# Prompt attention: the causal mask added in PSUM by VectorE, and a unit's reciprocal placed behind the next unit's maximum

## The chip, the core and the metric

The kernel runs on one core of a Trainium2 chip. The metric is the device time of one execution in microseconds; the figure of a kernel is the median of its runs. The core has five engines with queues of their own, which are released by semaphores: TensorE (PE, with its weight loads shown apart as PEld), VectorE (DVE), ScalarE (ACT), GpSimd (POOL) and SyncE (SP, which here starts DMAs).

## What is computed

One inference step of a decoder trunk of two layers, for a prompt of 512 tokens and for 8 samples of 8 tokens. The change touches one piece of it: the attention of the prompt over its own keys. With 512 tokens both the selected-block branch (all 8 blocks of 64 are selected) and the window branch (window 512) are plain causal attention:

```python
s = jnp.einsum('bcqgnd,bcsgd->bcqgns', qb, kb) * (HEAD_DIM ** -0.5)
p = masked_softmax(s, mask)      # mask: key position <= query position

def masked_softmax(s, mask):
    s = jnp.where(mask, s.astype(jnp.float32), -jnp.inf)
    m = jnp.max(s, axis=-1, keepdims=True)
    e = jnp.exp(s - m)
    return e / jnp.maximum(jnp.sum(e, axis=-1, keepdims=True), 1e-30)
```

There are 8 query heads in 2 groups (v = 0, 1) of 4 (g), and head size 64. The probabilities are multiplied by a gate per head and token, and the two branches are summed.

## The kernel before

The program is a row of blocks; all engines meet at the end of each. Each of the two layers has one block for the prompt attention. Its work is cut into NA = 32 units, `AU`: query tile t (128 queries, from 3 down to 0), branch b (0 selected, 1 window) and g (0 to 3). A unit holds both head groups v, and t + 1 key tiles, so w = 512, 384, 256 or 128 keys for t = 3, 2, 1, 0; eight units in a row have the same t. The units are numbered 0 to 31 here.

Every engine has its own hand-written order, one pass of a loop per unit n:

- PE: `scores(n)`, two fp32 matmuls (L1346) into banks 2(n mod 2) and 2(n mod 2) + 1, then two bf16 matmuls of the identity with the causal mask (L1348), which add the mask onto the last 128 columns of each bank; then `turn_probs(n - 3)`, which transposes the probabilities of the unit three back (L1359, LAG = 3); then `values(n - 4)`, the product with V (L1373). `scores(n)` waits for the exponentials of unit n - 2, which free its banks. `turn_probs(m)` waits for the scaled probabilities of m, and for the copies out of the transposes of m - 1.
- DVE: the negated maximum of both groups in one reduction (L1448), once the scores are there; then the copy of the transposes of unit n - 3 for v = 1 (L1405); then the wait for both exponentials of unit n, and the reciprocal of their sums (L1453).
- ACT: two exponentials with their sums (L1424) behind the maximum; then the copy of the transposes of n - 3 for v = 0 (L1405); every eighth unit the copy of the finished output (L1433).
- POOL: behind the reciprocal, two multiplications of the probabilities by reciprocal and gate (L1323).
- SP in this block only starts loads for the next one.

`cst` is the tile of constants in SBUF; `ident16` and `causal16` are bf16 views of it. `step(engine, instruction, name)` issues an instruction that raises a semaphore at its end, and makes the same engine wait for it before it goes on. The names in rows: `bank` is PSUM, and `R` is a large tile that holds queries, keys, probabilities and their sums.

Of the kernel before, what the change touches and what calls it, by code (L numbers as in the profile page):

```python
# [20 lines left out]

F32 = mybir.dt.float32
F32R = mybir.dt.float32r
BF16 = mybir.dt.bfloat16
I32 = mybir.dt.int32
U32 = mybir.dt.uint32
ALU = mybir.AluOpType
# [3 lines left out]
P = 128  # L31
# [13 lines left out]
NKV = 2  # L45
# [18 lines left out]
NEG = -1e30  # L64
# [5 lines left out]
CONST_W = {}  # L70


def _halved(a):

    return (np.asarray(a, np.float32).view(np.uint32) >> 16).astype(np.uint16).view(np.float32)


def _constants():

    cols = []  # L80

    def put(name, a):
        a = np.asarray(a, np.float32).reshape(a.shape[0], -1)
        full = np.zeros((P, a.shape[1]), np.float32)
        full[:a.shape[0]] = a
        CONST_W[name] = (sum(c.shape[1] for c in cols), a.shape[1])
        cols.append(full)

    i = np.arange(P)
    put("ident", np.eye(P))  # L90
    put("ones", np.ones((P, P)))
    put("ones64", (i[:, None] // HD == i[None] // HD))

    put("ident16", _halved(np.eye(P)))
    put("causal16", _halved(np.where(i[None] > i[:, None], NEG, 0.0)))
    put("hgmask", (i[:, None] // CH == i[None] // CH) & (i[:, None] <= i[None]))
    j = np.arange(NS)
    put("hgmask8", (j[:, None] // DT == j[None] // DT) & (j[:, None] <= j[None]))
    pos = np.concatenate([np.arange(SEQ), PAST + np.tile(np.arange(DT), NB), np.zeros(P - NS)]).astype(np.float32)
    inv = (np.float32(10000.0) ** (-np.arange(HD // 2, dtype=np.float32) / np.float32(HD // 2))).astype(np.float32)  # L100
    ang = (pos[:, None] * inv[None]).astype(np.float32).reshape(TT, P, HD // 2).transpose(1, 0, 2)
    put("cos", np.cos(ang.astype(np.float64)))
    put("sin", np.sin(ang.astype(np.float64)))
    c = np.arange(NCP)
    q = np.arange(SEQ).reshape(NT, P).T
    seen = (c[None, None] * CST + 2 * CST - 1 <= q[:, :, None]) & (c < NCP - 1)
    put("cmpneg", np.where(seen, 0.0, NEG))
    put("cmp01", seen)

    rows = np.arange(P)  # L110
    par_, hd, t = rows // (NH * DT), rows // DT % NH, rows % DT
    own = np.arange(NB // 2)[None, :, None, None] * 2 + par_[:, None, None, None] == np.arange(NB)[None, None, :, None]
    new = own & (np.arange(DT)[None, None, None] <= t[:, None, None, None])
    put("newneg", np.where(new, 0.0, NEG))
    put("winneg", np.where(np.arange(DT)[None] > t[:, None], 0.0, NEG))
    put("groupsum", (rows[:, None] // (NG * DT) == rows[None] // (NG * DT)) & (t[:, None] == t[None]))

    put("rowsel", j[:, None] % (2 * DT) == (par_ * DT + t)[None])
    put("pair", j[:, None] // (2 * DT) == np.arange(NB // 2)[None])
    put("head", hd[:, None] == np.arange(NH)[None])  # L120
    put("blkidx", np.tile(np.arange(16), (P, 1)))
    put("batch", (i[:, None] // DT % 4 == np.arange(4)[None]))
    n = np.arange(N)
    put("scan", np.tile(np.where(n < SEQ, n % CH != 0, (n - SEQ) % DT != 0), (P, 1)))
    return np.concatenate(cols, axis=1)
# [10 lines left out]
def build(nc, x_prompt, x_sample, cache_nsa_kv, cache_win_kv, state_hgrn, page_table,  # L136
# [4 lines left out]
    with ExitStack() as ctx:  # L141
# [56 lines left out]
        def const(name, rows=P):  # L198
            o, w = CONST_W[name]
            return cst[0:rows, o:o + w]  # L200

        ident, ones, ones64 = const("ident"), const("ones"), const("ones64")
        ident16, causal16 = const("ident16").bitcast(BF16), const("causal16").bitcast(BF16)

        G_ATTN, G_MLP, G_HG, G_KC, P_B1, P_LBA, P_OM, P_LNOM, P_HB = 0, 8, 16, 17, 18, 22, 26, 30, 34

# [319 lines left out]
        def layer(l):  # L526
# [663 lines left out]
            NA = len(AU)  # L1190
# [108 lines left out]
            with nc.Block() as block:  # L1299
# [26 lines left out]
                @block.tensor  # L1326
                def _(pe):
                    for u, (k, t) in enumerate(TURNS):
                        r, n, dst = turn_views(k, t)
                        if u >= 4:  # L1330
                            pe.wait_ge(sem(f"turn_kept{u % 2}"), (u - 4) // 2 + 1)
                        for g in range(n):
                            src = (q_tok, QR)[k][0:r, t, g * P:(g + 1) * P] if k < 2 else ktok[g][0:r, t, :]
                            ins = pe.transpose(bank[u % 4][:, g * r:(g + 1) * r], src, ident[0:r, 0:r])
                        ins.then_inc(sem("turned"), 1)
                    for i in range(2):
                        pe.wait_ge(sem(f"turn_kept{i}"), kept_before(len(TURNS), i))

                    def scores(n):
                        t, b, g = AU[n]  # L1340
                        w = (t + 1) * P
                        if n >= 2:
                            pe.wait_ge(sem("probs_made"), 2 * (n - 1))
                        for v in range(NKV):
                            k = slice(v * HD, (v + 1) * HD)
                            pe.matmul(bank[2 * (n % 2) + v][:, 0:w], QT[k, g, t * P:w], KT[k, b, 0:w], start=True, stop=False)  # L1346
                        for v in range(NKV):
                            ins = pe.matmul(bank[2 * (n % 2) + v][:, t * P:w], ident16, causal16,  # L1348
                                            start=False, stop=True)
                        ins.then_inc(sem("scored"), 1)  # L1350

                    def turn_probs(n):
                        t, b, g = AU[n]
                        for v in range(NKV):
                            pe.wait_ge(sem("probs_scaled"), 2 * n + v + 1)
                            if n >= 1:
                                pe.wait_ge(sem(f"probsT_kept{v}"), n)
                            for j in range(t + 1):
                                ins = pe.transpose(bank[4 + v][:, j * P:(j + 1) * P],  # L1359
                                                   probs[n % 4][:, v * 512 + j * P:v * 512 + (j + 1) * P], ident)  # L1360
                            ins.then_inc(sem(f"probs_turned{v}"), 1)

                    def values(n):
                        t, b, g = AU[n]
                        i = NT - 1 - t
                        if b == 0 and g == 0 and i >= 2:
                            pe.wait_ge(sem("o_kept"), i - 1)
                        for v in range(NKV):
                            pe.wait_ge(sem(f"probsT_kept{v}"), n + 1)
                        for j in range(t + 1):  # L1370
                            for v in range(NKV):

                                ins = pe.matmul(bank[6 + i % 2][v * HD:(v + 1) * HD, g * P:(g + 1) * P],  # L1373
                                                vtok[b][:, j, v * HD:(v + 1) * HD],
                                                probsT[n % 2][:, v * 512 + j * P:v * 512 + (j + 1) * P],
                                                start=(b == 0 and g == 0 and j == 0), stop=(b == 1 and j == t),
                                                skip_group_check=True)
                        ins.then_inc(sem("valued"), 1)

                    for n in range(NA + LAG + 1):  # L1380
                        if n < NA:
                            scores(n)
                        if LAG <= n < NA + LAG:
                            turn_probs(n - LAG)
                        if n > LAG:
                            values(n - LAG - 1)
# [50 lines left out]
                def _(dve):  # L1437
# [5 lines left out]
                    for n in range(NA + LAG):  # L1443
                        if n < NA:
                            w = (AU[n][0] + 1) * P
                            dve.wait_ge(sem("scored"), n + 1)
                            both = psum[:, n % 2 * 1024:n % 2 * 1024 + 1024].rearrange("p (v k) -> p v k", v=NKV)[:, :, 0:w]
                            dve.tensor_reduce(nmax[:, 2 * n:2 * n + 2], both, AX, ALU.max, negate=True).then_inc(sem("maxed"), 1)  # L1448
                        if n >= LAG:
                            keep_probsT(nc.vector, n - LAG, 1)  # L1450
                        if n < NA:
                            dve.wait_ge(sem("probs_made"), 2 * n + 2)
                            dve.reciprocal(rinv[:, 2 * n:2 * n + 2], rsum[:, 2 * n:2 * n + 2]).then_inc(sem("rsum_inverted"), 1)  # L1453

            att_scope.close()
            cmp_scope = ExitStack()
# [1021 lines left out]
```

## Time and profile before

| | us |
|---|---|
| median of 3 runs | 2060.67 |
| lowest and highest of them | 2057.65, 2062.05 |
| the profiled execution, its whole time | 2054.93 |
| its span, first to last instruction | 2053.1 |
| its attention of layer 0, first scores to the last unit's | 265.7 to 344.2 |
| its attention of layer 1, first scores to the last unit's | 1276.0 to 1354.4 |

The profiled execution lasted 2054.93 us, 1.8 us over its span and 5.7 us under the median. A row of the timeline gives the start, the duration, the engine, the line, the operation with its tiles, and in brackets how long the engine sat idle before it and what ended that. PE rows merge several matmuls; the end of a matmul is modelled. One fp32 matmul shows as two records.

### The profile page before, as it was taken

The page shows a single profiled execution, that of the slowest core. Times are in us where ns is not written, and L with a number is a line of the kernel's source. Part 1 is how long each engine was busy: PE and PEld are TensorE (multiplying, and loading weights), DVE is VectorE, ACT ScalarE, POOL GpSimd, SP SyncE. Part 2 cuts the span into 40 slices and gives each one's busy share as a digit, 9 for nine tenths or more (in the row PEclk, how much of TensorE's full clock was granted, in tenths as well). Part 3 has the DMA queues.
Part 4 walks back from the last instruction along what each step waited for, and adds up shares of the span by engine and source line. Part 5 has one row for each costly group of instructions (what it writes and reads, how often), then busy time and mean ns, then how long its engine had stood idle before and what let it go on. Part 6 is the DMA issues. An engine that isn't in the chain of part 4 may idle for free. (4 is left out here: it accounts for less than half of the span.)

```text
span 2053.1 us, 38910 instructions
## 1 busy us (share of the span) xinstructions
PE 1905.8 (93%) x15789; PEld 1785.9 (87%) x15789; DVE 1138.6 (55%) x1899; ACT 828.1 (40%) x1809; POOL 692.3 (34%) x470
## 2 busy tenths in 40 slices
PE   6999798988799999999999997989887999999998
PEld 6999555988599999999999984668875999999998
DVE  4589655454455555555528886555535454545454
ACT  4594355353534131313146923544435341313130
POOL 2325435240043333333323542443201333333331
PEclk8999888999999999999999997999999999999999
DMA  4220520432522222222222223222254222222221
GB/s 155 86 80 23 164 66 9 117 93 70 158 83 83 83 83 84 82 87 83 78 85 84 63 73 104 58 64 67 83 154 111 83 71 93 78 92 81 85 82 48
DMA packets 200638, 175.80 MB, mean 86 GB/s; under 512 B 11356, under 2 KB 198030, under 8 KB 200334
## 3 DMA queue, kind: packets, MB, share of 16 engines
q1 hardware_dynamic: 200354, 173.30, 27.7%
q8 instruction: 126, 2.06, 0.4%
q14 instruction: 50, 0.41, 0.1%
q10 hardware_dynamic: 108, 0.03, 0.0%
HBM read 162.67 MB, written 10.62 MB: 84 GB/s over the span
## 5 line engine op out<-in xcount | busy, mean ns | idle before, releaser
L427 POOL TENSOR_TENSOR WX<-RAW,WX 128x2048 fp32r<-128x2048 f32 (+2 forms) x48 | 222.4, 4634 | 523.0 <-ACT WX L423 523.0
L2391 DVE TENSOR_TENSOR sq<-sq 128x288 f32<-128x288 f32 x128 | 156.9, 1231 | 196.8 <-ACT sq L2360 196.8
L427 POOL TENSOR_TENSOR m_wl<-RAW,m_wh 128x2048 fp32r<-128x2048 f32 x36 | 166.5, 4624 | 285.1 <-ACT m_wh L423 285.1
L439 PE MATMUL bank<-UH,m_wl 128*128 128x288 f32 x640 | 188.7, 295 | 0.0
L438 PE MATMUL bank<-UL,m_wh 128*128 128x288 f32 x640 | 188.7, 295 | 0.0
L437 PE MATMUL bank<-UH,m_wh 128*128 128x288 f32 x640 | 188.6, 295 | 0.0
L439 PE MATMUL bank<-UH,WX 128*128 128x288 f32 x576 | 170.0, 295 | 0.0
L438 PE MATMUL bank<-UL,WX 128*128 128x288 f32 x576 | 169.8, 295 | 0.0
L437 PE MATMUL bank<-UH,WX 128*128 128x288 f32 x576 | 169.6, 295 | 0.0
L2410 DVE TENSOR_TENSOR OT<-bank,rstd 128x288 f32<-128x288 f32 x128 | 58.2, 455 | 183.2 <-PE bank L439 183.2
L2413 DVE TENSOR_TENSOR XT<-XT,OT 128x288 f32<-128x288 f32 x128 | 156.3, 1221 | 4.4
L423 ACT ACTIVATE WX<-RAW 128x2048 fp32r<-128x2048 f32 (+1 forms) x48 | 92.0, 1917 | 160.8 <-PE bank L439 150.8
L1616 PE MATMUL bank<-FTS,W1S 128*128 128x256 f32 (+1 forms) x512 | 155.9, 305 | 0.0
L437 PE MATMUL bank<-m_ah,m_wh 128*128 128x288 f32 x512 | 151.3, 296 | 0.0
L439 PE MATMUL bank<-m_ah,m_wl 128*128 128x288 f32 x512 | 151.0, 295 | 0.0
L438 PE MATMUL bank<-m_al,m_wh 128*128 128x288 f32 x512 | 151.0, 295 | 0.0
L1618 PE MATMUL bank<-FTS,W1S 128*128 128x256 f32 (+1 forms) x512 | 150.5, 294 | 0.0
L1619 PE MATMUL bank<-FTS,W1S 128*128 128x256 f32 (+1 forms) x512 | 150.1, 293 | 0.0
L2360 ACT ACTIVATE sq<-bank 128x288 f32<-128x288 f32 x128 | 52.5, 410 | 233.7 <-PE bank L439 216.9
L423 ACT ACTIVATE m_wh<-RAW 128x2048 fp32r<-128x2048 f32 x36 | 68.7, 1908 | 166.7 <-PE bank L439 166.7
L439 PE MATMUL bank<-m_ah,WX 128*128 128x288 f32 x448 | 132.2, 295 | 0.0
L438 PE MATMUL bank<-m_al,WX 128*128 128x288 f32 x448 | 132.0, 295 | 0.0
(386 smaller groups left out, 5829.3 us busy)
## 6 DMA issues: line engine op xcount, KB each, us to landing
RAW<-in_w_up SPq DMA_DIRECT2D x32, 1024.0 KB, 5.4
RAW<-in_w_down SPq DMA_DIRECT2D x32, 1024.0 KB, 5.2
RAW<-in_w_in SPq DMA_DIRECT2D x20, 1024.0 KB, 5.3
R<-in_cache_nsa_kv SPq DMA_DIRECT2D x128, 64.0 KB
HT<-in_cache_nsa_kv SPq DMA_DIRECT2D x128, 64.0 KB, 2.6
RAW<-in_w_in SPq DMA_DIRECT2D x6, 1056.0 KB, 5.4
R<-in_cache_nsa_kv SPq DMA_DIRECT2D x48, 128.0 KB, 2.8
out<-R SPq DMA_DIRECT2D x10, 512.0 KB, 5.0
```

The source lines that it names most:

```text
L423: act.activation(S.granule(S.wh, i, w), S.granule(S.raw, i, w), ACT.Copy).then_inc(sem(S.name + "w_hi"), 1)
L427: eng.tensor_tensor(S.granule(S.wl, i, w)[:, chunks], S.granule(S.raw, i, w)[:, chunks], S.granule(S.wh, i, w)[:, chunks].bitcast(F32), AL ...
L437: pe.matmul(out, wh[:, c, cols], ah[:, c, n], start=(c == 0), stop=False)
L438: pe.matmul(out, wh[:, c, cols], al[:, c, n], start=False, stop=False)
L439: ins = pe.matmul(out, wl[:, c, cols], ah[:, c, n], start=False, stop=(c == KC - 1))
L1616: pe.matmul(out, W1H[:, s, c, cols], xh, start=first and (h == 0 or CU[w][1] == 0), stop=False, skip_group_check=True)
L1618: pe.matmul(out, W1H[:, s, c, cols], xl, start=False, stop=False, skip_group_check=True)
L1619: ins = pe.matmul(out, W1L[:, s, c, cols], xh, start=False, stop=last, skip_group_check=True)
L2360: act.activation(relu[n % 4], bank[2 + u % 6][:, 0:HALF], ACT.Relu).then_inc(sem("m_relued"), 1)
L2391: dve.tensor_tensor(relu[n % 4], relu[n % 4], relu[n % 4], ALU.mult).then_inc(sem("relu_squared"), 1)
L2410: dve.tensor_tensor(grown[n % 2], bank[2 + u % 6][:, 0:HALF], rstd[:, halves(s)], ALU.mult).then_inc(sem("m_added"), 1)
L2413: dve.tensor_tensor(x, x, grown[n % 2], ALU.add).then_inc(sem("m_grown"), 1)
```

## The change

The bf16 mask matmuls are gone from PE. In their place DVE adds an fp32 mask to the last 128 columns of both banks, in PSUM, before the maximum, with a wait for its own end between the two. The reciprocal of unit n - 1 now stands behind the maximum of unit n, and ahead of the copy of the transposes, where before the reciprocal of unit n closed its own pass. The constants keep their total width.

```diff
-    put("ident16", _halved(np.eye(P)))
-    put("causal16", _halved(np.where(i[None] > i[:, None], NEG, 0.0)))
+    put("causal", np.where(i[None] > i[:, None], NEG, 0.0))
...
                         for v in range(NKV):
                             k = slice(v * HD, (v + 1) * HD)
-                            pe.matmul(bank[2 * (n % 2) + v][:, 0:w], QT[k, g, t * P:w], KT[k, b, 0:w], start=True, stop=False)
-                        for v in range(NKV):
-                            ins = pe.matmul(bank[2 * (n % 2) + v][:, t * P:w], ident16, causal16,
-                                            start=False, stop=True)
+                            ins = pe.matmul(bank[2 * (n % 2) + v][:, 0:w], QT[k, g, t * P:w], KT[k, b, 0:w], start=True, stop=True)
                         ins.then_inc(sem("scored"), 1)
...
+                            own = both[:, :, w - P:w]
+                            step(dve, dve.tensor_tensor(own, own, const("causal").unsqueeze(1).to_broadcast([P, NKV, P]), ALU.add),
+                                 "dve_done")
                             dve.tensor_reduce(nmax[:, 2 * n:2 * n + 2], both, AX, ALU.max, negate=True).then_inc(sem("maxed"), 1)
+
+                        if 1 <= n <= NA:
+                            dve.wait_ge(sem("probs_made"), 2 * n)
+                            dve.reciprocal(rinv[:, 2 * n - 2:2 * n], rsum[:, 2 * n - 2:2 * n]).then_inc(sem("rsum_inverted"), 1)
                         if n >= LAG:
                             keep_probsT(nc.vector, n - LAG, 1)
-                        if n < NA:
-                            dve.wait_ge(sem("probs_made"), 2 * n + 2)
-                            dve.reciprocal(rinv[:, 2 * n:2 * n + 2], rsum[:, 2 * n:2 * n + 2]).then_inc(sem("rsum_inverted"), 1)
```

DVE at the start of the attention of layer 0, before: maximum and reciprocal of units 0 to 2, then maximum, copy and reciprocal of unit 3.

```order
L1448 TENSOR_REDUCE R_0<-bank 128x2
L1453 RECIPROCAL R_0<-R_0 128x2
L1448 TENSOR_REDUCE R_0<-bank 128x2
L1453 RECIPROCAL R_0<-R_0 128x2
L1448 TENSOR_REDUCE R_0<-bank 128x2
L1453 RECIPROCAL R_0<-R_0 128x2
L1448 TENSOR_REDUCE R_0<-bank 128x2
L1405 COPY R_0<-bank 128x512
```

The same place after the change (L1438 the mask, L1440 the maximum, L1444 the reciprocal, L1393 the copy):

```order
L1438 TENSOR_TENSOR bank<-bank,cst 128x2x128
L1440 TENSOR_REDUCE R_0<-bank 128x2
L1438 TENSOR_TENSOR bank<-bank,cst 128x2x128
L1440 TENSOR_REDUCE R_0<-bank 128x2
L1444 RECIPROCAL R_0<-R_0 128x2
L1438 TENSOR_TENSOR bank<-bank,cst 128x2x128
L1440 TENSOR_REDUCE R_0<-bank 128x2
L1444 RECIPROCAL R_0<-R_0 128x2
L1438 TENSOR_TENSOR bank<-bank,cst 128x2x128
L1440 TENSOR_REDUCE R_0<-bank 128x2
L1444 RECIPROCAL R_0<-R_0 128x2
L1393 COPY R_0<-bank 128x512
```

Unit 1's maximum no longer stands behind unit 0's reciprocal, and so not behind unit 0's exponentials.

PE in the attention of layer 0, units 4 and 5, before (scores, mask, transposes, values):

```order
L1346 MATMUL bank<-R_0 128x512 x2
L1348 MATMUL bank<-cst 128x128 x2
L1359 MATMUL bank<-cst,R_0 128x128 x8
L1373 MATMUL bank<-R_0 64x128 x8
L1346 MATMUL bank<-R_0 128x512 x2
L1348 MATMUL bank<-cst 128x128 x2
```

And after:

```order
L1337 MATMUL bank<-R_0 128x512 x2
L1347 MATMUL bank<-cst,R_0 128x128 x8
L1361 MATMUL bank<-R_0 64x128 x8
L1337 MATMUL bank<-R_0 128x512 x2
```

Scores, transposes and values keep their order; only the mask matmuls are missing.

## Rows read from the trace of the kernel before

**Rows 1.** The page, part 1: engine, busy us (share of the span), instructions.
```profile
PE 1905.8 (93%) x15789; PEld 1785.9 (87%) x15789; DVE 1138.6 (55%) x1899; ACT 828.1 (40%) x1809; POOL 692.3 (34%) x470
```

**Rows 2.** Line L1348 alone: count, duration in ns min/median/max, first and last start.
```profile
L1348 PE MATMUL bank<-cst x128: 218/229/315, 266.8 to 1354.9; 128*128 128x128 bf16 x128
```

**Rows 3.** The timeline, layer 0, units 5 to 8 (t = 3), all engines.
```profile
284.28 1.13 PE L1346 MATMUL bank<-R 64*128 64x512 f32 x4
285.34 0.29 PE L1348 MATMUL bank<-cst 128*128 128x128 bf16 x2
285.59 1.06 PE L1359 MATMUL bank<-cst,R 128*128 128x128 f32 x8
285.66 1.22 DVE L1448 TENSOR_REDUCE R<-bank 128x2 f32<-128x1024 f32 x1 [0.50 <-PE bank L1348]
286.80 0.68 DVE L1405 COPY R<-bank 128x512 f32<-128x512 f32 x1
286.92 0.69 ACT L1424 ACTIVATE R<-bank,R 128x512 f32<-128x512 f32 x1 [1.47 <-DVE R L1448]
...
288.26 0.59 ACT L1405 ACTIVATE R<-bank 128x512 f32<-128x512 f32 x1
...
288.97 0.86 PEld L1359 LDWEIGHTS bank<-cst,R 128*128 128x128 f32 x8 [0.19 <-issue]
289.00 1.07 PE L1359 MATMUL bank<-cst,R 128*128 128x128 f32 x8
...
291.02 0.92 PE L1346 MATMUL bank<-R 64*128 64x384 f32 x4
```

**Rows 4.** The same, units 29 to 31 (t = 0).
```profile
341.14 0.49 PE L1346 MATMUL bank<-R 64*128 64x128 f32 x4
...
341.89 0.42 DVE L1448 TENSOR_REDUCE R<-bank 128x2 f32<-128x256 f32 x1
...
343.05 0.27 ACT L1405 ACTIVATE R<-bank 128x128 f32<-128x128 f32 x1
...
343.46 0.43 PE L1359 MATMUL bank<-cst,R 128*128 128x128 f32 x2
...
344.19 0.49 PE L1346 MATMUL bank<-R 64*128 64x128 f32 x4
```

**Rows 5.** DVE adds a constant to PSUM data, then reduces it behind a wait for itself.
```profile
403.42 0.42 DVE L1935 TENSOR_TENSOR R<-bank,cst 128x256 f32<-128x256 f32 x1
403.87 0.42 DVE L1936 TENSOR_REDUCE R<-R 128x8 f32<-128x256 f32 x1
```

**Rows 6.** The timeline, layer 0, the first units and unit 5's scores.
```profile
269.94 1.20 DVE L1448 TENSOR_REDUCE R<-bank 128x2 f32<-128x1024 f32 x1
...
272.65 0.17 DVE L1453 RECIPROCAL R<-R 128x2 f32<-128x2 f32 x1 [1.51 <-ACT R L1424]
...
272.68 2.08 PE L1346 MATMUL bank<-R 64*128 64x512 f32 x4 [1.45 <-ACT R L1424]
272.74 1.20 DVE L1448 TENSOR_REDUCE R<-bank 128x2 f32<-128x1024 f32 x1
...
275.54 1.20 DVE L1448 TENSOR_REDUCE R<-bank 128x2 f32<-128x1024 f32 x1
...
280.87 1.13 PE L1346 MATMUL bank<-R 64*128 64x512 f32 x4
```

**Rows 7.** The page, part 5: busy us, mean ns of one, idle before and its releaser.
```profile
L2413 DVE TENSOR_TENSOR XT<-XT,OT 128x288 f32<-128x288 f32 x128 | 156.3, 1221 | 4.4
```

**Rows 8.** Stretches of the span: length, busy us of PE, PEld, DVE, ACT, POOL, then granted TensorE clock, DMA.
```profile
345.00:346.00 1.00, 0.72 (x6) 0.36 (x6) 0.65 (x2) 0.60 (x3) 0.79 (x2) 1.00 0.00 0
346.00:347.00 1.00, 0.49 (x2) 0.32 (x2) 0.17 (x1) 0.51 (x4) 0.50 (x2) 0.84 0.00 0
347.00:348.00 1.00, 1.00 (x6) 0.50 (x6) 0.29 (x1) 0.14 (x1) 0.38 (x1) 0.50 0.06 16
543.60:547.00 3.40, 2.45 (x20) 1.83 (x20) 0.00 (x0) 3.40 (x7) 0.00 (x0) 1.00 0.83 187
```

More of the change, by code:

```diff
@@ L23 @@
 F32R = mybir.dt.float32r
-BF16 = mybir.dt.bfloat16
 I32 = mybir.dt.int32
@@ L70 @@
 CONST_W = {}
-def _halved(a):
-    return (np.asarray(a, np.float32).view(np.uint32) >> 16).astype(np.uint16).view(np.float32)
 def _constants():
@@ L202, in build @@
         ident, ones, ones64 = const("ident"), const("ones"), const("ones64")
-        ident16, causal16 = const("ident16").bitcast(BF16), const("causal16").bitcast(BF16)
         G_ATTN, G_MLP, G_HG, G_KC, P_B1, P_LBA, P_OM, P_LNOM, P_HB = 0, 8, 16, 17, 18, 22, 26, 30, 34
```

## The prediction, made before the changed kernel ran

> **What bounds the kernel now.** I read the page's busy shares first. PE is busy for 93% of the span and DVE for 55% [rows 1]. That invites the reading that anything taken off PE and given to DVE is a gain, so the next question is whether PE is what ends the waits in the one stage that changes. The stage is the attention, twice some 78 us from the first scores to the last unit's scores, 32 units each.
>
> The timeline of four units with t = 3 answers it [rows 3]. Follow one unit. Its scores start at 284.28. Its mask matmuls start at 285.34 and end at 285.63, and the maximum starts 0.03 later, at 285.66. It ends at 286.88; the exponentials start at 286.92. ACT's copy of the transposes stands behind them in its queue: 288.26 to 288.85. The next transposes on PE wait for that copy, since it frees their bank, and start at 289.00, 0.15 after its end, with 0.19 us of idle before the weight load. Transposes and values run to 291.02, where the scores two units on start. So there is a **loop over two units**: scores, mask, maximum, exponentials, ACT's copy, then transposes and values on PE. It takes 4.72 + 2.02 = 6.74 us, 3.37 per unit. PE's own work is just under it: its waits in the loop are of the order of 0.1 us.
>
> With t = 0 it is the same [rows 4]: scores at 341.14, maximum at 341.89, ACT's copy 343.05 to 343.32, the transposes 0.14 later at 343.46, and the scores two units on at 344.19: 3.05 us for two units. PE and the loop are nearly in balance, and the loop is the longer one. What counts is therefore the latency from scores to exponentials, not the work on PE.
>
> **The change part by part.**
>
> *The mask matmuls go.* There are 128 records of about 0.23 us, one for each v of 64 units [rows 2]. On PE a unit gives back the 0.25 us from the mask's start to the transposes' start (285.34 to 285.59) [rows 3]. On the loop it is a little less: DVE can start 0.04 after the end of the scores' own matmuls. For t = 3 these end at 284.28 + 1.13 = 285.41, so DVE starts at 285.45 in place of 285.66, 0.21 earlier. For t = 0 they end at 341.63, so DVE starts at 341.67 in place of 341.89, 0.22 earlier [rows 4]. I take 0.215.
>
> *The add comes.* It is 256 fp32 elements per partition, one input from PSUM and one from the constants. The trace has that instruction in another stage: 0.42 us, and the reduction that waits for it starts 0.45 after its start [rows 5]. That one writes to SBUF; no DVE row of before writes to PSUM. From above, the dearest row for adding so little is 1.22 us for 288 elements, with both inputs in SBUF while POOL is at work [rows 7]; the add has one input in PSUM, so I take the row of the same shape, 0.45. From below, if the maximum could start as early as the copy does behind a maximum that it need not wait for, 0.08 before its end (286.80 against 286.88) [rows 3], the pair would cost 0.42 - 0.08 = 0.34. The loop thus grows by 0.45 - 0.215 = **0.235 us per two units**, with ends of 0.125 and about 1.0.
>
> A rule bears on the lower end. The Trainium skill, "VectorE: DVE Perf Modes", section "The DRAIN you can't avoid", says that a semaphore between chained VectorE operations costs nothing extra. Here a waited-for pair has a gap of 0.03 and a pair without a wait an overlap of 0.08, so the rows differ from the rule by 0.11. By the rule the loop would grow by 0.125.
>
> *What the freed PE time is worth.* In the new loop PE has 0.25 less per unit and the loop is 0.12 more, so PE waits longer and nothing is gained. DVE stays clear: for t = 3 it has 0.45 + 1.22 + 0.17 + 0.68 = 2.52 us of 3.49; for t = 0 0.45 + 0.42 + 0.17 + 0.29 = 1.33 of 1.64.
>
> *The reciprocal moves.* In the steady part the old wait was over by the time the next scores came, so nothing is gained there, but with scores 0.2 earlier it would have begun to hold the add; the move keeps that from happening. Queued behind the new wait on unit n - 1's exponentials is only DVE's copy, and these exponentials ended long before. POOL gets its reciprocal about 2 us later for t = 3 and 1 us later for t = 0; the transposes that need its result come three units later, so this is covered.
>
> *The head of the stage* is where the move pays. In units 0 to 3 the maxima start at 269.94, 272.74 and 275.54, 2.80 apart: maximum, exponentials, reciprocal, maximum in a row, the last reciprocal starting at 272.65 [rows 6]. Now unit n + 1's maximum runs beside unit n's exponentials. By hand: unit 0's maximum starts at 267.35, unit 1's at 269.03 (was 269.94), unit 2's at 271.7 (272.74), and unit 3's scores at 271.75 in place of 272.68. They ran at half the clock (2.08 us where 1.13 is usual); at that price they end at 273.83, and unit 3's maximum starts at 274.3 in place of 275.54. Its exponentials and ACT's copy end at 277.6, so the second set of transposes starts at 277.75, and unit 5's scores come at 279.8 to 280.3 in place of 280.87 [rows 6]. One loop later, at unit 7, 0.35 to 0.85 is left: I take 0.6. Had the clock been full, it would be up to 1.5.
>
> *Sum for a layer.* From unit 7 to unit 31 are 12 loops: 12 x 0.235 = 2.8. The last unit's own mask adds 0.24. Less 0.6 at the head: +2.45. The drain of the last three units and the next stage, which starts at a meeting of all engines, shift with it. SP's loads end long before. Two layers: **+4.9 us**. On the profiled execution that is 2054.93 + 4.9 = 2059.8; on the median, 2060.67 + 4.9 = 2065.6. A measurement of this kernel can tell about 0.2% (4.1 us) from no change, so this is just past it.
>
> **The rivals.**
>
> *PE is the bound after all.* Then each unit gives back 0.25: 64 x 0.25 = 16 us, 2044.7. For it speaks 93% [rows 1]; against it the start 0.15 after ACT's copy, at t = 3 and t = 0 alike [rows 3, 4].
>
> *The head gives back the rest.* With full clock at the head, 1.5 us come back per layer: 2 x (3.04 - 1.5) = 3.1, so 2063.7. The pair at 0.34 gives the like: 12 x 0.125 + 0.13 - 0.6 = 1.0 per layer, 2062.7. Both are within 0.2%. That second figure is what the page's rule, named above, would give.
>
> *The clock falls among the units of t = 0.* PE now has some 1.15 us of work in 1.64. Before, the granted clock fell to half behind two microseconds with 0.72 and 0.49 of PE busy [rows 8]. At half clock PE needs 2.1 us for such a unit, 0.45 more than the loop. This decides once PE's share there is too low. Eight units in two layers: 16 x 0.45 = 7.2 more, 2072.8. Against it: a stretch of 3.4 us with 2.45 busy kept the full clock [rows 8].
>
> *The add into PSUM is dear.* At 1.22 plus 0.03 the loop grows by 1.03, 0.8 more than taken: 25 loops x 0.8 = 20 us, 2085. It is decided by the add's own duration, above about 0.5.
>
> **How the numbers follow.** The forecast has 0.62, with a range of its own of 2062.5 to 2069; a third of that chance, 0.21, is within 0.2%. The head or the cheap pair 0.16, the clock 0.12, the dear add 0.04, PE as the bound 0.06. Faster by over 0.2%: 0.06. Within 0.2%: 0.21 + 0.16 = 0.37. Slower: 0.41 + 0.12 + 0.04 = 0.57. The range leaves out PE as the bound and the dear add (0.10) and some tails: 2059 to 2073.5.
>
> **What the new profile would show.** The add at 0.42 with the maximum 0.45 behind its start; the scores of t = 3 some 6.97 us apart over two units and those of t = 0 3.29; the transposes still 0.14 behind ACT's copy, with longer PE waits; maxima at the head nearer than 2.8; unit 31's scores about 2.2 us later. PE spacings that shrink by 0.25 per unit would make the prediction wrong, as would a granted clock of half in the units of t = 0.

## The result, and the profile after

The changed kernel takes 2067.92 us in the median of 8 runs (2063.28 to 2074.19), the kernel before 2059.57 (8 runs, 2056.84 to 2065.17). The ratio is 1.0037 with a 95% interval of 1.0021 to 1.0053, so the change costs 7.6 us by the ratio (4.3 to 10.9); the two medians are 8.4 apart. The forecast was 4.9 more: the direction and the range were right, the size was under the measured one.

The page of the profiled execution (2063.28 us, span 2061.5), part 1, against [rows 1]:

```profile
span 2061.5 us, 38718 instructions
PE 1896.4 (92%) x15661; PEld 1783.1 (86%) x15661; DVE 1157.5 (56%) x1963; ACT 828.8 (40%) x1809; POOL 693.5 (34%) x470
```

PE has 128 instructions and 9.4 us fewer, DVE 64 instructions and 18.9 us more. Next the add and the maximum, each line alone (count, ns min/median/max, first and last start):

```profile
L1438 DVE TENSOR_TENSOR bank<-bank,cst x64: 411/433/433, 270.8 to 1361.0; 128x256 f32<-128x256 f32 x64
L1440 DVE TENSOR_REDUCE R<-bank x64: 424/824/1226, 271.3 to 1361.5; 128x2 f32<-128x1024 f32 x16, 128x2 f32<-128x768 f32 x16, 128x2 f32<-128x512 f32 x16, 128x2 f32<-128x256 f32 x16
```

The loop over two units at t = 3, to be read against [rows 3]: units 6 to 8 of layer 0.

```profile
285.80 1.13 PE L1337 MATMUL bank<-R 64*128 64x512 f32 x4
...
286.98 0.43 DVE L1438 TENSOR_TENSOR bank<-bank,cst 128x256 f32<-128x256 f32 x1 [0.76 <-PE bank L1337]
...
287.45 1.22 DVE L1440 TENSOR_REDUCE R<-bank 128x2 f32<-128x1024 f32 x1
...
288.59 0.15 DVE L1444 RECIPROCAL R<-R 128x2 f32<-128x2 f32 x1
...
288.71 0.69 ACT L1412 ACTIVATE R<-bank,R 128x512 f32<-128x512 f32 x1 [1.17 <-DVE R L1440]
...
290.05 0.59 ACT L1393 ACTIVATE R<-bank 128x512 f32<-128x512 f32 x1
290.75 0.86 PEld L1347 LDWEIGHTS bank<-cst,R 128*128 128x128 f32 x8 [0.76 <-POOL R L1314]
290.79 1.07 PE L1347 MATMUL bank<-cst,R 128*128 128x128 f32 x8
...
292.81 0.92 PE L1337 MATMUL bank<-R 64*128 64x384 f32 x4
```

The add starts 1.18 us after the scores' start, the maximum 0.47 later, ACT's copy ends at 290.64, and the transposes start 0.15 behind it. The releaser printed beside them is POOL, but POOL's result of that time belongs to a later unit; what ended 0.15 before is the copy, as in [rows 3]. From 285.80 to 292.81 are 7.01 us, where it was 6.74. At t = 0 the scores of units 28 and 30 start at 344.18 and 347.49, 3.31 apart, where [rows 4] has 3.05.

Where the time went, by stretches of the span (the length, then busy us of PE, PEld, DVE, ACT, POOL, the granted TensorE clock, DMA). The changed kernel: the stage ahead of layer 0's attention, that attention from first to last scores, its drain up to the next stage's first matmul, and the same two for layer 1.

```profile
218.22:269.64 51.42, 38.76 (x380) 28.19 (x381) 34.34 (x105) 18.47 (x75) 16.84 (x25) 0.73 0.42 128
269.64:349.41 79.77, 65.34 (x577) 41.66 (x577) 54.28 (x120) 46.04 (x153) 36.16 (x59) 1.00 0.16 45
349.41:357.97 8.56, 5.56 (x34) 2.87 (x33) 2.98 (x12) 3.75 (x14) 3.15 (x9) 0.66 0.00 0
1280.69:1360.50 79.81, 65.39 (x576) 41.69 (x577) 54.27 (x120) 46.08 (x153) 36.20 (x59) 1.00 0.16 44
1360.50:1369.11 8.61, 5.61 (x34) 2.86 (x33) 2.60 (x11) 3.67 (x13) 3.08 (x9) 0.61 0.01 3
```

And the same five of the kernel before:

```profile
218.40:265.73 47.33, 34.82 (x380) 25.05 (x381) 34.27 (x105) 18.43 (x75) 16.80 (x25) 0.82 0.45 138
265.73:344.19 78.46, 73.89 (x638) 45.98 (x639) 43.90 (x89) 45.89 (x153) 36.39 (x60) 0.96 0.16 45
344.19:352.63 8.44, 5.89 (x36) 2.99 (x34) 2.74 (x11) 3.81 (x14) 2.69 (x8) 0.65 0.01 2
1276.00:1354.44 78.44, 73.95 (x638) 46.00 (x638) 43.96 (x89) 45.77 (x151) 36.39 (x60) 0.96 0.16 45
1354.44:1361.38 6.94, 4.33 (x36) 2.53 (x35) 2.73 (x11) 3.92 (x15) 2.70 (x8) 1.00 0.01 4
```

The two attentions with their drains are 1.31 + 0.12 + 1.37 + 1.67 = 4.5 us longer. The spans differ by 8.4. The first row alone is 4.1 longer, in code that is the same in both kernels: it ran at a granted clock of 0.73 here and 0.82 there. Later stretches add and take smaller amounts. The same stage ahead of layer 1's attention, first in the changed kernel and then in the one before, shows that this goes with the execution and not with the kernel:

```profile
1232.84:1280.69 47.85, 35.33 (x381) 25.11 (x381) 34.32 (x105) 18.47 (x75) 16.74 (x25) 0.82 0.44 137
1227.41:1276.00 48.59, 35.94 (x381) 25.68 (x381) 34.28 (x105) 18.44 (x75) 16.74 (x25) 0.79 0.43 134
```

In layer 1 the changed kernel is the quicker one there, and its own two layers differ by 3.6 us.

### The profile page after: what moved, and what is told of

Same layout as the page of the kernel before. It is cut to its first block and busy times, and to the rows that moved or that the text cites. A ratio compares the mean times of both kernels' runs of the same rounds, so it can differ in the third digit from the quotient of the medians.

```text
span 2061.5 us, 38718 instructions
## 1 busy us (share of the span) xinstructions
PE 1896.4 (92%) x15661; PEld 1783.1 (86%) x15661; DVE 1157.5 (56%) x1963; ACT 828.8 (40%) x1809; POOL 693.5 (34%) x470
```

## The experiments

The theory: the attention runs at the pace of the loop over two units (scores, mask, maximum, exponentials, ACT's copy, transposes, values), and what the change does to that latency is what it costs. The rivals: PE's work is the bound; the order of the reciprocal or the missing PE work (by way of the clock) makes the difference; DVE's own load is the bound.

"Attention" in the table is first to last scores in layers 0 and 1, "drain" from the last scores to the next stage's first matmul, both of the profiled execution, and "head" is unit 0 to unit 5 in layer 0. The ratio is to the kernel before as timed beside the same kernels, so the median of the kernel before is given as a range.

| kernel | median us | ratio to before (95%) | head | attention | drain |
|---|---|---|---|---|---|
| before | 2059 to 2061 | 1 | 15.14 | 78.46, 78.44 | 8.44, 6.94 |
| changed | 2067.92 | 1.0037 (1.0021 to 1.0053) | 13.06 | 79.77, 79.81 | 8.56, 8.61 |
| recip_only | 2054.55 | 0.9967 (0.9956 to 0.9979) | 12.23 | 75.58, 75.58 | 7.97, 6.94 |
| mask_only | 2074.97 | 1.0083 (1.0068 to 1.0098) | 16.79 | 84.02, 84.50 | 8.27, 8.92 |
| ones_dve | 2072.42 | 1.0061 (1.0046 to 1.0075) | 14.48 | 83.87, 83.86 | 8.29, 8.06 |
| add_twice | 2082.34 | 1.0116 (1.0099 to 1.0132) | 15.34 | 88.37, 88.63 | 9.42, 9.41 |
| no_mask | 2051.38 | 0.9954 (0.9932 to 0.9975) | 11.80 | 72.51, 73.63 | 6.73, 6.74 |
| act_first_dve | 2043.73 | 0.9932 (0.9918 to 0.9946) | 12.85 | 69.29, 69.29 | 6.54, 6.52 |
| act_first_pe | 2044.31 | 0.9929 (0.9916 to 0.9942) | 13.34 | 71.41, 73.14 | 6.68, 6.69 |
| act_first_recip_pe | 2042.37 | 0.9917 (0.9900 to 0.9934) | 11.47 | 69.54, 69.54 | 6.29, 6.28 |

**The reciprocal alone (recip_only).** From the kernel before:

```diff
+                        if 1 <= n <= NA:
+                            dve.wait_ge(sem("probs_made"), 2 * n)
+                            dve.reciprocal(rinv[:, 2 * n - 2:2 * n], rsum[:, 2 * n - 2:2 * n]).then_inc(sem("rsum_inverted"), 1)
                         if n >= LAG:
                             keep_probsT(nc.vector, n - LAG, 1)
-                        if n < NA:
-                            dve.wait_ge(sem("probs_made"), 2 * n + 2)
-                            dve.reciprocal(rinv[:, 2 * n:2 * n + 2], rsum[:, 2 * n:2 * n + 2]).then_inc(sem("rsum_inverted"), 1)
```

> The kernel before with one edit: a unit's reciprocal stands behind the next unit's maximum, the mask stays on PE. Loop theory: the steady part does not change (3.37 us per unit at t = 3), only the head of the attention gets shorter, by about 2 us at unit 7 in each layer, since the maxima no longer stand behind the exponentials of the unit before: 4 us less in all, 2056. Rival, that the move buys nothing on its own and the changed kernel's shorter head comes from the missing mask matmuls: 0. The rest of the changed kernel's loss over the attention's own would then lie in the mask's move alone.

It is 6.8 us faster than before (4.3 to 9.1), where 4 was expected. The attentions are 2.9 us shorter each. DVE at the head:

```profile
268.49 2.50 DVE L1448 TENSOR_REDUCE R<-bank 128x2 f32<-128x1024 f32 x2 [1.53 <-PE bank L1348]
271.24 0.17 DVE L1451 RECIPROCAL R<-R 128x2 f32<-128x2 f32 x1 [0.24 <-ACT R L1424]
272.64 1.23 DVE L1448 TENSOR_REDUCE R<-bank 128x2 f32<-128x1024 f32 x1 [1.24 <-PE bank L1348]
```

Two maxima run back to back, and the reciprocal comes behind them; in [rows 6] each maximum had to wait for the reciprocal. The scores of units 5 and 7 are still 6.74 apart, so the steady part is unchanged, and the gain in the attentions is in the first units: unit 7 comes 18.97 us after unit 0, before 21.88. The rival (no gain of its own) falls.

Not all of these 2.9 us are the order's. In the kernel before, unit 3's scores ran at half clock, 2.08 us in [rows 6]; here they took 1.13:

```profile
272.59 1.13 PE L1346 MATMUL bank<-R 64*128 64x512 f32 x4
```

At full clock on both sides the order is worth 1.87 us a layer: unit 7 comes 19.70 after unit 0 in layer 0 of act_first_pe and 17.83 in act_first_recip_pe, two kernels further down that differ in the reciprocal alone. Layer 1 of act_first_pe, with unit 3's scores at 2.08 us, needs 21.43. So about 1.9 of the 2.9 is the order, as expected, and about 1.0 the clock. The kernel before shows the half clock at unit 3 in both layers and recip_only in neither; whether the order brings that about was not shown.

**The mask alone (mask_only).** The changed kernel with the reciprocal put back:

```diff
-                        if 1 <= n <= NA:
-                            dve.wait_ge(sem("probs_made"), 2 * n)
-                            dve.reciprocal(rinv[:, 2 * n - 2:2 * n], rsum[:, 2 * n - 2:2 * n]).then_inc(sem("rsum_inverted"), 1)
                         if n >= LAG:
                             keep_probsT(nc.vector, n - LAG, 1)
+                        if n < NA:
+                            dve.wait_ge(sem("probs_made"), 2 * n + 2)
+                            dve.reciprocal(rinv[:, 2 * n:2 * n + 2], rsum[:, 2 * n:2 * n + 2]).then_inc(sem("rsum_inverted"), 1)
```

> The changed kernel with the reciprocal back in its old place, so only the mask moves. Loop theory: the loop over two units grows by 0.26 us (12 times in a layer, 3.1 us), the four units at the head each carry the add's 0.47 in a row with maximum, exponentials and reciprocal (1.9 us), and for t = 0 that row, 0.47 + 0.42 + 0.04 + 0.70 + 0.05 + 0.17 = 1.85 us per unit, becomes longer than half the loop of 1.65 (with t = 1 about 2.4 us in a layer). Together 7.4 us a layer, 15 us in all: 2074. Rival, the order of the reciprocal does not matter for the steady part: 3.1 + 1.9 a layer, 10 us in all.

It is 17 us slower than before (14 to 20), where 15 was expected and 10 by the rival. The attentions alone do not bear the theory out so well: they are 5.6 and 6.1 us longer, for 7.4 expected and 5.0 by the rival. The head costs the 1.9 that was put for it (unit 7 comes 23.79 us after unit 0, before 21.88), and from unit 7 to unit 31 it is 3.6 and 4.1 us more than before, for 5.5 and 3.1. Its units of t = 0 show the row of work that the rival left out:

```profile
343.54 0.17 DVE L1446 RECIPROCAL R<-R 128x2 f32<-128x2 f32 x1 [0.53 <-ACT R L1412]
343.62 0.41 DVE L1438 TENSOR_TENSOR bank<-bank,cst 128x256 f32<-128x256 f32 x1
...
344.07 0.42 DVE L1440 TENSOR_REDUCE R<-bank 128x2 f32<-128x256 f32 x1
```

DVE waits for the exponentials, inverts, and only then begins the next unit's add. The last steps of layer 0 show its length: the scores of units 29 to 31 come 1.83 apart, for 1.85 expected, where two units of the changed kernel take 3.31. But this row rules only part of the stage. From unit 7 to unit 31 it adds 0.5 us in layer 0 and 1.0 in layer 1 to the changed kernel's time (60.22 and 60.71 against 59.71 and 59.76), not 2.4, and in layer 1 the clock had part in it: over the last 8 us before unit 31 it was 0.84. So of the change's two halves the mask costs about 17 us and the reciprocal's move gives back 6.8 alone and about 9 once the add is there; of these 9, 3.7 us a layer are at the head (23.79 against 20.06 at unit 7), where mask_only again ran unit 3's scores at half clock.

**Its cost apart from PE (ones_dve).** From recip_only, with the mask still on PE:

```diff
+                            own = both[:, :, w - P:w]
+                            step(dve, dve.tensor_tensor(own, own, const("ones").unsqueeze(1).to_broadcast([P, NKV, P]), ALU.mult),
+                                 "dve_done")
                             dve.tensor_reduce(nmax[:, 2 * n:2 * n + 2], both, AX, ALU.max, negate=True).then_inc(sem("maxed"), 1)
```

> The mask stays on PE and the reciprocal is moved (as in recip_only); on top, DVE multiplies the last 128 columns of both banks by one in PSUM before the maximum, an instruction of the shape and cost of the changed kernel's add that changes no value. It parts the cost of the instruction on DVE from the relief of PE. Loop theory: the loop over two units grows by 0.47, 12 times a layer and once more at the end, 6.1 us a layer with about 0.5 at the head: 13 us over recip_only, 2068. Rival, that the missing mask matmuls on PE had something to do with the changed kernel's loss (a lower clock, say): less than 10 over recip_only.

It is 18 us over recip_only by the medians, for 13 expected. Units 5 and 7 are 7.20 apart (283.52 to 290.72), and 6.74 + 0.47 is 7.21. Most of the 5 us that were not expected is at the head: unit 7 comes 21.68 us after unit 0, against 18.97 in recip_only, 2.7 us a layer where 0.5 was put. Two things are in it. One is the clock, since unit 3's scores ran at half of it:

```profile
275.25 2.08 PE L1346 MATMUL bank<-R 64*128 64x512 f32 x4 [0.25 <-ACT R L1424]
```

The other is the add. In layer 0 of the changed kernel and of no_mask, below, where these scores took 1.13 us in both, one add puts unit 7 back by 1.73 us (20.06 against 18.33). So the expectation was 1.2 too low for the head by itself, because most of the first units run at the pace of the chain and carry the add in full; the other 1.0 goes with the clock (an estimate from these two differences). PE's relief plays no part in the steady loop: with PE as loaded as before, the instruction costs at least as much as in the changed kernel. The rival falls.

**Twice the cost, and none (add_twice, no_mask).** From the changed kernel:

```diff
                             step(dve, dve.tensor_tensor(own, own, const("causal").unsqueeze(1).to_broadcast([P, NKV, P]), ALU.add),
                                  "dve_done")
+                            step(dve, dve.tensor_tensor(own, own, const("causal").unsqueeze(1).to_broadcast([P, NKV, P]), ALU.add),
+                                 "dve_done")
```

> The changed kernel with the mask added twice, each with its own wait (a masked score gets -2e30 in place of -1e30). Loop theory: another 0.47 on the loop, 6.1 us a layer and about 0.5 at the head: 13 us over the changed kernel, 2081. Rival, DVE has room and hides it: under 3 us more.

no_mask takes both lines out instead of doubling them, so it leaves out the causal mask.

> The changed kernel without the add: no causal mask in the prompt attention at all, the one part of the computation left out. Loop theory: the loop shrinks by 0.47 against the changed kernel, to 6.52 at t = 3, still over PE's two units of about 6.2: 13 us less than the changed kernel, 2055, and some 5 us less than the kernel with mask on PE and reciprocal moved by the attention's own time, 2050. The two figures differ by the 3 us or so that the changed kernels lose outside the attention's rows; which is nearer tells whether that loss goes with the mask's place or with the DVE instruction. Rival, DVE's add costs nothing on the path: 2068.

add_twice measures 14.4 us over the changed kernel (13 expected), no_mask 16.5 under it. That is nearer to the 18 than to the 13 of its two routes, but its runs go from 2041.11 to 2055.9, and its attentions and drains alone are 17.1 shorter, so the two are not told apart. Units 5 and 7 are 7.46 apart with two adds (283.80 to 291.26), 7.00 with one (282.70 to 289.70), 6.53 with none (282.33 to 288.86): **0.46 to 0.47 per add, in a straight line**. In the attention of layer 0 DVE is busy for 41.9 of 72.5 us with no add, 54.3 of 79.8 with one and 66.8 of 88.4 with two. It has room in all three, so it isn't its load that counts but its place in the chain.

**The loop cut open (act_first_dve, act_first_pe).** The copy on ACT is moved, in the changed kernel and in the one before:

```diff
                     for n in range(NA + LAG + 2):
+                        if LAG <= n < NA + LAG:
+                            keep_probsT(nc.scalar, n - LAG, 0)
                         if n < NA:
                             w = (AU[n][0] + 1) * P
                             act.wait_ge(sem("maxed"), n + 1)
...
-                        if LAG <= n < NA + LAG:
-                            keep_probsT(nc.scalar, n - LAG, 0)
```

> The changed kernel with one edit on ACT: its copy of the transposes of unit n - 3 stands ahead of the exponentials of unit n, no longer behind them. Loop theory: this cuts the loop open (transposes no longer wait behind exponentials), so PE becomes the bound, at about 3.08 us per unit for t = 3, 2.46 for t = 2, 1.85 for t = 1, and about 1.4 for t = 0 where DVE bounds: some 8 us less than before in each layer, 2043 in all, and the mask off PE is then a gain. Rival, DVE's own load or the add in PSUM is what costs: the place of ACT's copy changes nothing and the time stays 8 us over before.

> The kernel before with the same edit on ACT, mask on PE. Loop theory: PE's own work was only 0.04 to 0.1 us per unit under the loop, so PE bounds at once at 3.30 to 3.33 us per unit (t = 3): 1 to 3 us a layer at most, 2055 to 2059 in all. With act_first_dve this tells what the mask costs on PE once PE is the bound: 0.25 x 64 = 16 us. Rival, that ACT's copy behind the exponentials is not what holds the transposes: no change.

act_first_dve came out at 2043.73, for 2043 expected; its attentions take 69.29 us, 10.5 less than the changed kernel's. The place of one instruction on ACT is worth 24 us of a kernel in which PE is 92% busy, and units of t = 3 now come 3.11 apart, for 3.08 expected. This is the strongest evidence for the loop.

act_first_pe was a **miss**: 2044.31, where 2055 to 2059 was expected. It has the order of act_first_dve, with the mask on PE. Layer 0, unit 6:

```profile
286.24 0.28 PE L1348 MATMUL bank<-cst 128*128 128x128 bf16 x2
286.31 0.86 PEld L1359 LDWEIGHTS bank<-cst,R 128*128 128x128 f32 x8
286.36 1.04 PE L1359 MATMUL bank<-cst,R 128*128 128x128 f32 x8
```

From the mask's start to the transposes' start are 0.12 us, where [rows 3] has 0.25 (285.34 to 285.59). Its units of t = 3 are 3.18 us apart; act_first_dve's are 3.11. So the mask costs PE 0.07 us per unit at t = 3, not 0.25: in the kernel before, ACT's copy had ended only 0.14 before the transposes at 285.59, and 0.13 of the 0.25 was PE waiting for it. The wait does not show as idle time there, because the mask matmuls' modelled ends reach over it. PE's own work was thus 0.19 under the loop, not 0.04 to 0.1.

**Both orders, mask on PE (act_first_recip_pe).** recip_only with ACT's copy moved in the same way:

> The kernel before with both orders changed and the mask left on PE: ACT's copy ahead of the exponentials, and the reciprocal behind the next maximum. Loop theory: the steady part is PE-bound as in act_first_pe (3.18 us per unit at t = 3), and the head gains what recip_only gained, 2 to 2.9 us a layer: 4 to 6 us under act_first_pe, 2039. Rival, both edits shorten the same thing and do not add: 2044.

2042.37 us, 0.9917 of before (0.9900 to 0.9934): the lowest median here, 17 us under the kernel before and 26 under the changed one. Against act_first_pe the medians show 1.9 us, where 4 to 6 was expected and none by the rival, so they lie nearer the rival. The attentions are 1.9 us shorter in layer 0, at full clock in both, which is what the reciprocal gave; in layer 1 they are 3.6 shorter, because act_first_pe had half clock at unit 3 there. One unit at t = 3:

```profile
287.72 0.29 PE L1348 MATMUL bank<-cst 128*128 128x128 bf16 x2
...
287.84 1.04 PE L1359 MATMUL bank<-cst,R 128*128 128x128 f32 x8
288.04 1.22 DVE L1448 TENSOR_REDUCE R<-bank 128x2 f32<-128x1024 f32 x1 [1.30 <-PE bank L1348]
288.49 0.60 ACT L1405 ACTIVATE R<-bank 128x512 f32<-128x512 f32 x1 [0.91 <-PE bank L1359]
...
289.30 0.69 ACT L1426 ACTIVATE R<-bank,R 128x512 f32<-128x512 f32 x1 [0.22 <-DVE R L1448]
```

ACT copies while DVE still looks for the maximum, and sat idle for 0.91 us before: the time was free. Against act_first_dve (2043.73, attentions 69.29) there is no difference that these runs can tell. With the loop open, these runs no longer show which engine had better add the mask.

## Why the prediction was right, and where it was not

*The loop bounds the stage, not PE.* Right: the loop's length followed the add in steps of 0.47 (no_mask, changed, add_twice), and moving ACT's copy removed it. The first rival, PE as the bound, is refuted; its price of 16 us was also wrong, since PE's part of the mask is 0.07 us per unit at t = 3. "Of the order of 0.1 us" for PE's waits was too small: 0.19 per unit at t = 3.

*The mask matmuls give the loop 0.215.* Right: scores to add are 1.18 us at t = 3 (1.17 worked out).

*The add with its wait costs 0.45.* A little low: 0.47. Into PSUM it takes 433 ns, where the instruction of the same shape into SBUF, [rows 5], has a median of 417. The loop grew by 0.27 at t = 3, not 0.235, and from unit 7 to unit 31 by 3.13 us in layer 0, for 2.8. The lower end, 0.34, is refuted here: each add with its wait moved the maximum by 0.47, more than its own 0.43. The Trainium skill, "VectorE: DVE Perf Modes", section "The DRAIN you can't avoid", says that the semaphore costs nothing extra. No run has the add without its wait, so that was not tested on this pair; of other pairs, the reciprocal, which has no wait for the maximum, starts at 288.59, 0.08 before the maximum's end at 288.67. The upper end is refuted too: the longest add took 433 ns. It had rested on a mean, the 1.22 us of [rows 7], of instructions from 0.46 (the median) to 4.50 us.

*What the freed PE time is worth: nothing.* Right for the loop, by ones_dve. But the step that gave PE back "0.25 us from the mask's start to the transposes' start" was mis-sized: act_first_pe shows 0.12 between those starts, and 0.07 per unit.

*The head gives back 0.6 us at unit 7.* Too low: 1.82 in layer 0 (20.06 us from unit 0 to unit 7, before 21.88). The term took unit 3's scores at half clock, 2.08 us as in [rows 6]. In the changed kernel they ran at the full one:

```profile
274.04 1.13 PE L1337 MATMUL bank<-R 64*128 64x512 f32 x4 [2.41 <-ACT R L1412]
...
275.63 1.13 PE L1337 MATMUL bank<-R 64*128 64x512 f32 x4 [0.47 <-ACT R L1412]
```

The granted clock over the attention was 1.00 against 0.96 before. The prediction had named this case as a rival, with up to 1.5; so that rival's condition came true. Layer 1 of act_first_pe, with unit 3 at half clock, came 1.73 later at unit 7 than its layer 0, so the clock is enough for the 1.2 that were missed.

*The drain shifts with the rest.* Wrong for layer 1: 8.61 us at a clock of 0.61, before 6.94 at 1.00. The transposes (x2 each) no longer take the 0.42 us of the row ahead:

```profile
1361.13 0.42 PE L1347 MATMUL bank<-cst,R 128*128 128x128 f32 x2
1361.48 0.44 PE L1361 MATMUL bank<-R 128*64 128x128 f32 x4
...
1362.67 0.28 ACT L1393 ACTIVATE R<-bank 128x128 f32<-128x128 f32 x1
...
1363.09 0.66 PE L1347 MATMUL bank<-cst,R 128*128 128x128 f32 x2 [1.16 <-POOL R L1314]
```

These start 0.14 behind ACT's copy, as in the loop, and 2.59 us after unit 31's scores, where it was 2.33 before. That 0.26 is the last unit's own mask, 0.24 in the sum; the rest, about 1.4, came with the clock, which fell while PE stood idle for 1.2 us. The kernel before shows the same price with the same code: its drain took 8.44 us at a clock of 0.65 in layer 0, 6.94 at 1.00 in layer 1. The rival had put the fall among the units of t = 0; there the clock stayed full (1.00 over both attentions), though PE was busy for only 65 of 80 us. In a slower kernel it did come there, in mask_only's layer 1.

*The sum.* 4.9 was forecast, and 4.5 is seen in the attentions and drains of the two profiled executions. That these are so close is luck. Two errors cancelled: the head gave back 2.4 us more than was put, in both layers together, against a loop too cheap by 0.7 and drains too cheap by 1.3. The loop's part is the mechanism and was sound; the head and the drains went with the clock, which the sum had wrong in both places.

*What stays open.* The runs say 7.6, with 4.3 to 10.9, and 4.5 lies at the low end. The part of the span outside attentions and drains went from 1880.8 us (before) to 1894.5 (no_mask) over these profiled executions, with the same code, so a single pair cannot settle 3 us. Taken from the medians less the attentions of the profile, it averages 1886.4 for the five kernels with the mask on PE and 1888.4 for the five without; that is within the scatter of either group (1884.6 to 1888.9, and 1884.7 to 1890.3). Whether any of it belongs to the change was not shown.

## What to carry to other kernels

Before moving work off the busiest engine, follow one unit through all engines and find which wait starts it again: here a loop over two units, with PE 93% busy, set the pace, and 0.47 us put on it cost a quarter of a microsecond per unit. Look also at the clock in the rows that you compare: a head with one unit's scores at half clock looks like a dearer chain. When such a loop runs through an engine's queue, look for an instruction in it that is ready early but stands behind a late one; moving that copy ahead on ACT was worth 16 us with the mask on PE and 24 with it on DVE, where the change itself cost 7.6. Idle time printed at PE can be too small: 0.25 us between the starts of two matmul groups, which looked like work, was half wait.

## What the runs showed of the hardware

- An add of 256 fp32 elements per partition in place in PSUM, with a constant from SBUF, takes 433 ns on DVE, 16 more than the like into SBUF (medians); its successor behind a wait starts 0.47 us after it.
- The same code gets a different clock from layer to layer of one execution: the stage ahead of the attention took the changed kernel 51.4 us at 0.73 in layer 0 and 47.9 at 0.82 in layer 1. One profile of each kernel does not resolve differences of 4 us outside the stage that was changed.
- Half clock at the scores of unit 3 put unit 7 of act_first_pe back by 1.73 us, layer 1 against layer 0; in the kernel before, a drain at 0.65 took 8.44 us and one at 1.00 took 6.94.
